# Five moves in a two-layer transformer kernel: the masks' load, one unit of an output projection, a residual add, a weight part, and a set of logarithms

## The chip, the cores and the metric

The kernel runs on one core of one Trainium2 chip. Its time is the device time of one execution in microseconds (us). The kernel before was timed in three runs: 1099.5, 1100.54 and 1105.1 us, median 1100.54 us. A further execution, recorded by the hardware profiler, is the one from which every duration below is read. Of the engines, TensorE (PE) multiplies matrices, VectorE (DVE) and ScalarE (ACT) work on elements, GpSimd (POOL) helps in one phase, and SyncE (SP) issues nearly all transfers (DMA).

## The reference, cut to what matters

Two transformer blocks run one after the other on 256 tokens of width 1024. What the change touches is, in the first block, the projections of the normed input, the cross-attention with its output projection and residual, and, in the second block, the forget gates of a gated linear recurrence:

```
h = rms_norm(x, mix_norm_g)
(..., f_q, f_k, f_v, f_g, s_q, s_k, s_v, gate_logits) = split_proj(h @ w_in)   # start of block 1
...
x = x + merged @ w_mix_out
q = rms_norm(x) @ w_xq ; k, v = rms_norm(mem) @ w_xkv          # 4 heads of 256
x = x + concat_h(softmax(q k^T / 16) v) @ w_xo                  # output projection "xo", residual
x = x + swiglu(rms_norm(x, ffn_norm_g), w_gate, w_up, w_down)   # feed-forward "a"
...
z = rms_norm_2(x) @ w_in_2                                      # start of block 2
f = lb + (1 - lb) * sigmoid(zf) ; logf = log(max(f, tiny)) ; k = (1 - lb) * sigmoid(-zf)
o = hgrn2_direction(q, k, v, logf)                              # forward and backward
```

The kernel computes the recurrence in levels; at levels 1 to 32 it merges scores under a 0/1 mask (`masks`, seven squares of 128x128), and this is the only use of the masks.

## The kernel before, in words

Every weight matrix is cut into **units**, at most 128 x 2048 floats (1 MB) each, numbered in the order in which they are used: fq 0 to 3, fk 4 and 5, fv 6 and 7, fg 8, sq 9 and 10, skv 11, cc 12 and 13, and so on. A unit passes through four engines. SP loads it into one of three `raw` buffers (`fetch`, L408), which is allowed when DVE has finished with unit n-3. ACT rounds it to a high part `whi` (`hi`, L1146), after PE has finished unit n-3. DVE subtracts to get the low part `wlo` (`lo`, L1717). PE then multiplies high by high, high by low and low by high (L531 for feature-major results, L588 for token-major ones, L633 and L635 for the first pair of a feed-forward). Activations are split into high and low parts in the same way (`ha`, `ox_hi`, `ox_lo`).

There is no scheduler. Each engine has a list of instructions written out by hand (`sync`, `tensor`, `scalar`, `vector`, `gpsimd`) and works through it in order; semaphores connect the five lists. On ACT and DVE a call such as `hi(U["xo0"][0][0] + 2)` stands two units ahead of PE, so it splits unit xo0 first half + 2, that is xo0's second half (the units of xo0 and xo1 alternate: xo0/0, xo1/0, xo0/1, xo1/1, then the feed-forward's first gate piece and first up piece).

The places of the change:

- **Start.** SP issues 448 KB of masks (`mk`, L433) behind many small loads and ahead of units 3 and 4. DVE turns them into bytes (`masks`, L1808) before the split of unit 8.
- **Cross-attention.** PE transposes the probabilities of head h (`x_probs`, L864), ACT copies them out (`xpt`), PE multiplies them with V (`x_values`, L876), ACT and DVE split the result (`ox_hi` L1345, `ox_lo` L1739). `x_values(2)` also needs the second half of V, which ACT copies out of PSUM (L1191) when PE has finished `mv1`. A unit of the first half of xo needs heads 0 and 1 only, one of the second half also heads 2 and 3.
- **Residual.** `add_half` adds the two halves of a PSUM bank to X (L1958) and then makes the low part of the next input (L1727). The feed-forward's first matmul (L633) waits for the low part of the first two rows of X, `("xo", 0)`.
- **Gates of block 2.** ACT computes sigmoids (L1491, L1492), scales the keys (L1499), loads another table and takes three logarithms for each of two directions (`half_logs`, L1505 to L1507). DVE does `half_gate` (L2108 to L2116) ahead of them and `half_log` (L2121) behind them. In between stand splits of the units hq0, zv and zu.

Of the kernel before, what the change touches and what calls it, by code (L numbers as in the profile page):

```python
# [95 lines left out]
def build(nc, d, out):  # L96
# [20 lines left out]
    masks = at("masks", [P, 7, P], U8, 91)  # L117
# [282 lines left out]
    def sync(e):  # L400
# [9 lines left out]
        def fetch_for(*names):  # L410
            for name in names:
                for u, _, _ in U[name]:
                    fetch(u + 2 + RAW)
# [19 lines left out]
        e.dma_start(mk[:, :, :], d["c_masks"].rearrange("p (l n) -> p l n", l=7)).then_inc(s_mk, 16)  # L433
# [7 lines left out]
        fetch_for("fk", "fv")  # L441
# [61 lines left out]
    def tensor(e):  # L503
# [400 lines left out]
        x_probs(3)  # L904
        x_values(2)
        unit("xo0", 0, OX, 1, ox_ready, a_evac.on(("mv0", 1)))
# [229 lines left out]
    def scalar(e):  # L1136
# [200 lines left out]
        def x_probs(h):  # L1337
            e.wait_ge(*pe_turn.on(("cross", h)))
            if h >= 2:
                e.wait_ge(*pe_val.on(("cross", h - 2)))  # L1340
            e.activation(xPT[h % 2][:, :, :], Tb, ACT.Copy).then_inc(*a_soft.up(("xpt", h)))
# [22 lines left out]
        x_probs(3)  # L1364
        ox_hi(2)
        hi(U["xo0"][0][0] + 2)
# [167 lines left out]
        tables("natural_log_exp_and_others")  # L1534
        half_logs(0, 0)
        hi(U["hq0"][1][0] + 2)
# [174 lines left out]
    def vector(e):  # L1711
# [95 lines left out]
        e.wait_ge(s_mk, 16)  # L1807
        e.tensor_copy(masks[:, :, :], mk[:, :, :]).then_inc(*v_stat.up("masks"))  # L1808
# [77 lines left out]
        rows_of("mem", Rm, 3)  # L1886
        e.wait_ge(*v_stat.on("cumulated"))
# [66 lines left out]
        def add_half(name, linear, s, i, gain, bias_ready=None):  # L1954
            for j in range(2):
                r = X[:, 4 * i + 2 * j:4 * i + 2 * j + 2, :]
                e.wait_ge(*half(linear, j))
                e.tensor_tensor(r, wide(banks[s][:, 512 * j:512 * j + 512]), r, ALU.add).then_inc(  # L1958
                    *v_evac.up((name, 2 * i + j)))
            for g in (2 * i, 2 * i + 1):  # L1960
                e.wait_ge(*v_evac.on((name, g)))
                scaled_lo(name, HA, g, lambda k: X[:, 2 * g + k, :], gain)
# [53 lines left out]
        lo(U["mv1"][1][0] + 2)  # L2016
        ox_lo(2)
        lo(U["xo0"][0][0] + 2)
# [3 lines left out]
        lo(U["xo1"][1][0] + 2)  # L2022
        add_half("xo", "xo0", 1, 0, lambda c: g_col("ffn_norm_g", c))
# [163 lines left out]
        half_gate(0, 1)  # L2187
        half_log(0, 0)
        lo(U["hq0"][1][0] + 2)
# [293 lines left out]
```

## Time and profile before

| what | value |
|---|---|
| three timed runs, median | 1100.54 us |
| the profiled execution, its own time | 1103.07 us |
| its span, first to last instruction | 1101.0 us |
| PE busy | 1081.7 us, 98% |
| DVE, ACT, POOL busy | 755.7, 600.8, 52.4 us |
| granted TensorE clock, mean | 0.998 of full |
| HBM traffic | 165 GB/s over the span |

2.07 us of the profiled execution's time lie outside its span. A page of the profile gives busy time by engine, a busy share by slice, the chain of work that ended last, and groups of instructions. Behind it stand the views used below: the waits of one engine, the timeline of a stretch, stretches with busy time and granted clock (windows), and the list of transfers.

### The profile page before, as it was taken

Reading aid. Unit: us, or ns where it says so; the run is one execution under the profiler, and the core shown is the slowest. Engines: PE = TensorE matmul, PEld = TensorE weight load, DVE = VectorE, ACT = ScalarE, POOL = GpSimd, SP = SyncE. Lnnn points to the kernel's source line nnn. Section 1 sums busy time; section 2 is a strip of 40 time slices with the busy share of each in tenths; the row PEclk is TensorE's granted clock in tenths of the full one; section 3 lists DMA queues with packets and bytes.
Section 4 is the critical chain, followed back from the end, with each engine's and each line's share of the span. In section 5 each row is a group of like instructions: output and inputs, shape, how many; then the busy total and the mean of one; then the engine's idle time right before and its main releaser. Section 6 shows DMA issues by size and latency. Waiting matters only on the chain.

```text
span 1101.0 us, 17157 instructions
## 1 busy us (share of the span) xinstructions
PE 1081.7 (98%) x7340; PEld 987.7 (90%) x7340; DVE 755.7 (69%) x875; ACT 600.8 (55%) x719; POOL 52.4 (5%) x32
## 2 busy tenths in 40 slices
PE   8999999999999999999999999999999999999997
PEld 7988888999998988888889899999999888888886
DVE  5465765567645468777558897579947888776456
ACT  5533355543534365455455986588655665555443
POOL 0000000000000000000000151005300000000000
PEclk9999999999999999999999999999999999999999
DMA  9954244465454347555556455444444637664641
GB/s 307 218 169 134 95 139 131 134 211 191 155 195 142 122 156 247 181 191 182 172 182 192 124 181 155 132 155 135 153 154 132 203 119 226 191 191 154 211 152 39
DMA packets 140075, 183.14 MB, mean 166 GB/s; under 512 B 14036, under 2 KB 90304, under 8 KB 140000
## 3 DMA queue, kind: packets, MB, share of 16 engines
q1 hardware_dynamic: 139736, 181.73, 52.4%
q8 instruction: 58, 0.95, 0.4%
q10 hardware_dynamic: 264, 0.32, 0.1%
q14 instruction: 17, 0.14, 0.0%
HBM read 180.79 MB, written 1.25 MB: 165 GB/s over the span
## 4 chain that ended last, share of the span: by engine, by line
PE 87%; ACT 6%; DVE 4%; issue 2%; DMA 1%; SPq 0%; DVEq 0%; ACTq 0%
PE ps L531 34%; PE ps L557 22%; PE ps L559 11%; PE ps L588 5%; PE ps L965 3%; DVE wlo L1717 2%; ACT whi L1146 2%; PE ps L633 1%; DMA raw<-in_w_in 1%; PE ps L1094 1%; PE ps L779 1%; PE ps L754 1%; PE ps L635 1%; PE ps L766 1%; ACT ha L1682 1%
## 5 line engine op out<-in xcount | busy, mean ns | idle before, releaser
L1717 DVE TENSOR_TENSOR wlo<-raw,whi 128x2048 fp32r<-128x2048 f32 (+2 forms) x170 | 379.3, 2234 | 184.0 <-ACT whi L1146 183.7
L1146 ACT ACTIVATE whi<-raw 128x2048 fp32r<-128x2048 f32 (+1 forms) x169 | 313.2, 1857 | 84.6 <-PE ps L531 39.7
L531 PE MATMUL ps<-ha,whi 128*128 128x256 f32 (+1 forms) x1728 | 316.8, 285 | 1.7 <-DVE wlo L1717 1.7
L531 PEld LDWEIGHTS ps<-ha,whi 128*128 128x128 f32 (+1 forms) x1728 | 268.4, 191 | 9.0 <-issue 7.3
L531 PE MATMUL ps<-ha,wlo 128*128 128x256 f32 (+1 forms) x864 | 244.3, 283 | 0.0
L557 PE MATMUL ps<-ha,whi 128*128 128x512 f32 x640 | 224.7, 396 | 0.6 <-DVE wlo L1717 0.6
L559 PE MATMUL ps<-ha,wlo 128*128 128x256 f32 x640 | 179.4, 280 | 0.0
L531 PEld LDWEIGHTS ps<-ha,wlo 128*128 128x128 f32 (+1 forms) x864 | 164.9, 191 | 0.2
L557 PEld LDWEIGHTS ps<-ha,whi 128*128 128x128 f32 x640 | 120.0, 187 | 29.0 <-issue 0.9
L557 PE MATMUL ps<-pr,whi 128*128 128x512 f32 x352 | 123.3, 395 | 0.0
L559 PEld LDWEIGHTS ps<-ha,wlo 128*128 128x128 f32 x640 | 120.9, 189 | 0.1
L559 PE MATMUL ps<-pr,wlo 128*128 128x256 f32 x352 | 98.7, 280 | 0.0
L557 PEld LDWEIGHTS ps<-pr,whi 128*128 128x128 f32 x352 | 66.0, 187 | 15.5
L2421 POOL TENSOR_TENSOR xf<-xf,pf 128x512 f32<-128x512 f32 x14 | 31.3, 2234 | 743.0 <-DVE pb L2121 698.5
L559 PEld LDWEIGHTS ps<-pr,wlo 128*128 128x128 f32 x352 | 66.5, 189 | 0.0
L1399 ACT ACTIVATE silu<-silu 128x512 f32<-128x512 f32 x22 | 13.9, 632 | 61.8 <-DVE silu L2047 61.8
L588 PE MATMUL ps<-whi,ha 128*128 128x512 f32 x128 | 40.0, 394 | 0.6 <-DVE wlo L1717 0.6
L1394 ACT ACTIVATE silu<-ps 128x512 f32<-128x512 f32 x22 | 13.1, 597 | 41.9 <-PE ps L559 37.9
L965 PE MATMUL ps<-qt,kt 128*128 128x128 f32 x256 | 32.6, 282 | 1.9 <-DVE am L2158 1.9
L965 PEld LDWEIGHTS ps<-qt,kt 128*128 128x128 f32 x256 | 31.5, 198 | 2.4 <-issue 2.1
L2144 DVE TENSOR_TENSOR qt<-qt,q 128x1024 f32<-128x1024 f32 x16 | 28.1, 1756 | 3.5 <-ACT qt L1442 3.4
L588 PEld LDWEIGHTS ps<-whi,ha 128*128 128x128 f32 x128 | 23.5, 188 | 5.6 <-DVE wlo L1717 1.0
(377 smaller groups left out, 1770.7 us busy)
## 6 DMA issues: line engine op xcount, KB each, us to landing
raw<-in_w_in SPq DMA_DIRECT2D x55, 1024.0 KB, 5.3
raw<-in_w_ffn_gate SPq DMA_DIRECT2D x11, 1024.0 KB, 5.2
raw<-in_w_ffn_up SPq DMA_DIRECT2D x11, 1024.0 KB, 5.2
raw<-in_w_gate SPq DMA_DIRECT2D x11, 1024.0 KB, 5.1
raw<-in_w_up SPq DMA_DIRECT2D x11, 1024.0 KB, 5.1
raw<-in_w_xkv SPq DMA_DIRECT2D x8, 1024.0 KB, 5.0
raw<-in_w_ffn_down SPq DMA_DIRECT2D x8, 1024.0 KB, 5.0
raw<-in_w_down SPq DMA_DIRECT2D x8, 1024.0 KB, 5.0
```

The source lines that it names most:

```text
L531: mm = e.matmul(ps[0:width, m * T:(m + 1) * T], a[:, kk, m * width:(m + 1) * width], b[:, off + k, :], start=k == 0 and j == 0 and m % 2 = ...
L557: e.matmul(banks[s][:, at_:at_ + 512], wh[:, kk, c], H[2][:, :, k, :], start=k == 0, stop=False, skip_group_check=True)
L559: mm = e.matmul(banks[s][:, at_ + T:at_ + 512], wl[:, kk, c], H[0][:, k, :], start=False, stop=k == K - 1, skip_group_check=True)
L588: mm = e.matmul(banks[s][:, t * 512:t * 512 + ncol], b[:, k, t * P:(t + 1) * P], a[:, kk, 0:ncol], start=k == 0 and j == 0, stop=k == 7 an ...
L633: e.matmul(banks[ss[i]][:, at_:at_ + 512], wh[:, k, c], H[2][:, :, k, :], start=k == 0, stop=False, skip_group_check=True)
L965: mm = e.matmul(Sb[w][:, m * P:(m + 1) * P], Kt[b][:, m, w * P:(w + 1) * P], Q_[:, m, wq_ * P:(wq_ + 1) * P], start=m == 0, stop=True, ski ...
L1146: e.activation(h, r, ACT.Copy).then_inc(*hi_done.up(n))
L1394: e.activation(silu[w][:, :, :], split_sums(ss[2 * (i % 2)])[1], ACT.Copy).then_inc(*a_evac.up(f"{b}g{i}"))
L1399: e.activation(silu[w][:, :, :], silu[w][:, :, :], ACT.Silu).then_inc(*a_stat.up((f"silu {b}", i)))
L1717: e.tensor_tensor(l, r, h.bitcast(F32), ALU.subtract).then_inc(*lo_done.up(n))
L2144: e.tensor_tensor(Qt[b][:, :, :], Qt[b][:, :, :], q[:, :, :], ALU.mult).then_inc(*v_mix.up(("qt", i, n)))
L2421: e.tensor_tensor(Xfl, Xfl, Pfu[:, :, h - 1:h].broadcast_to(shp), ALU.add).then_inc(*p_mix.up(("xf", i, n)))
```

## The change: what it does

1. SP's load of the masks moves from ahead of unit 3 to between units 10 and 11. DVE's conversion to bytes moves from ahead of the split of unit 8 to just ahead of the first attention work (behind the copy `rm`, L1752).
2. On PE the first unit of the output projection (xo0/0) moves ahead of `x_values(2)`. On ACT and DVE the split of xo0/1 moves ahead of the split of head 2's result.
3. On DVE the split of the feed-forward's first up piece (two units behind xo1/1) moves from ahead of the first residual add to between the add and the low parts that follow it.
4. On ACT the split of unit zv/1 moves ahead of the first three logarithms, on DVE ahead of the first addition of logarithms.

No instruction is added or removed.

```diff
@@ sync
-        e.dma_start(mk[:, :, :], d["c_masks"].rearrange("p (l n) -> p l n", l=7)).then_inc(s_mk, 16)
         fetch(3)
         fetch(4)
...
-        fetch_for("fk", "fv")
+        fetch_for("fk")
+        e.dma_start(mk[:, :, :], d["c_masks"].rearrange("p (l n) -> p l n", l=7)).then_inc(s_mk, 16)
+        fetch_for("fv")
@@ tensor
         x_probs(3)
+        unit("xo0", 0, OX, 1, ox_ready, a_evac.on(("mv0", 1)))
         x_values(2)
-        unit("xo0", 0, OX, 1, ox_ready, a_evac.on(("mv0", 1)))
         x_values(3)
@@ scalar
         x_probs(3)
+        hi(U["xo0"][0][0] + 2)
         ox_hi(2)
-        hi(U["xo0"][0][0] + 2)
...
         tables("natural_log_exp_and_others")
+        hi(U["hq0"][1][0] + 2)
         half_logs(0, 0)
-        hi(U["hq0"][1][0] + 2)
@@ vector
-        e.wait_ge(s_mk, 16)
-        e.tensor_copy(masks[:, :, :], mk[:, :, :]).then_inc(*v_stat.up("masks"))
         lo_for("fv")
...
         rows_of("mem", Rm, 3)
+        e.wait_ge(s_mk, 16)
+        e.tensor_copy(masks[:, :, :], mk[:, :, :]).then_inc(*v_stat.up("masks"))
...
+            if between is not None:
+                lo(between)
             for g in (2 * i, 2 * i + 1):
...
+        lo(U["xo0"][0][0] + 2)
         ox_lo(2)
-        lo(U["xo0"][0][0] + 2)
         ox_lo(3)
         lo(U["xo1"][0][0] + 2)
         lo(U["xo0"][1][0] + 2)
-        lo(U["xo1"][1][0] + 2)
-        add_half("xo", "xo0", 1, 0, lambda c: g_col("ffn_norm_g", c))
+        add_half("xo", "xo0", 1, 0, lambda c: g_col("ffn_norm_g", c), U["xo1"][1][0] + 2)
...
         half_gate(0, 1)
+        lo(U["hq0"][1][0] + 2)
         half_log(0, 0)
-        lo(U["hq0"][1][0] + 2)
```

The order of SP's transfers at the start. `raw_50 128x4x512` is unit 4, the first half of fk; `128x4x64 x8` are units 9 and 10. Before:

```order
L432 DMA sc<-in_forget_bias 8x1 x2
L433 DMA mk<-c_masks 128x896
L408 DMA raw_49<-in_w_in 128x2x512
L408 DMA raw_50<-in_w_in 128x4x512
L408 DMA raw_51<-in_w_in 128x4x512
```

and in the changed kernel:

```order
L432 DMA sc<-in_forget_bias 8x1 x2
L408 DMA raw_49<-in_w_in 128x2x512
L408 DMA raw_50<-in_w_in 128x4x512
L408 DMA raw_51<-in_w_in 128x4x512
L439 DMA m_tm<-in_mem 128x2x512
L408 DMA raw_49<-in_w_in 128x4x512
L439 DMA m_tm<-in_mem 128x2x512
L408 DMA raw_50<-in_w_in 128x4x512
L408 DMA raw_51<-in_w_in 128x8x8 x2
L408 DMA raw_49<-in_w_in 128x4x64 x8
L408 DMA raw_50<-in_w_in 128x4x64 x8
L441 DMA mk<-c_masks 128x896
```

The masks (`mk`) now stand behind unit 10 instead of ahead of unit 3.

DVE from the end of the cross-attention to the feed-forward. `xres` rows are the residual adds, `ha` rows the low parts, `wlo` rows the splits of weights. Before:

```order
L1717 TENSOR_TENSOR wlo_57<-raw_51,whi_54 128x2048
L1739 TENSOR_TENSOR ox_lo<-ps,ox_hi 128x512
L1717 TENSOR_TENSOR wlo_55<-raw_49,whi_52 128x2048
L1739 TENSOR_TENSOR ox_lo<-ps,ox_hi 128x512
L1717 TENSOR_TENSOR wlo_56<-raw_50,whi_53 128x2048
L1717 TENSOR_TENSOR wlo_57<-raw_51,whi_54 128x2048
L1717 TENSOR_TENSOR wlo_55<-raw_49,whi_52 128x2048
L1958 TENSOR_TENSOR xres<-ps,xres 128x512 x2
L1727 SCALAR_TENSOR_TENSOR ha<-xres,gc,ha 128x256 x4
```

and in the changed kernel:

```order
L1718 TENSOR_TENSOR wlo_57<-raw_51,whi_54 128x2048
L1718 TENSOR_TENSOR wlo_55<-raw_49,whi_52 128x2048
L1740 TENSOR_TENSOR ox_lo<-ps,ox_hi 128x512 x2
L1718 TENSOR_TENSOR wlo_56<-raw_50,whi_53 128x2048
L1718 TENSOR_TENSOR wlo_57<-raw_51,whi_54 128x2048
L1959 TENSOR_TENSOR xres<-ps,xres 128x512 x2
L1718 TENSOR_TENSOR wlo_55<-raw_49,whi_52 128x2048
L1728 SCALAR_TENSOR_TENSOR ha<-xres,gc,ha 128x256 x4
```

The first two adds now stand ahead of the last split, and the two splits of head 2's and head 3's results follow each other.

ACT at the logarithms of block 2. `pf`, `qt_133`, `xf` are the first direction, `pb`, `qt_134`, `xb` the second, `whi_53` is unit zv/1. Before:

```order
L1499 ACTIVATE kb<-kb,sc 128x256 x4
L1164 ACT_TABLE_LOAD
L1505 ACTIVATE pf<-pf,sc 128x1024
L1506 ACTIVATE qt_133<-qt_133,sc 128x1024
L1507 ACTIVATE xf<-xf,sc 128x1024
L1146 ACTIVATE whi_53<-raw_50 128x2048
L1505 ACTIVATE pb<-pb,sc 128x1024
L1506 ACTIVATE qt_134<-qt_134,sc 128x1024
L1507 ACTIVATE xb<-xb,sc 128x1024
```

and in the changed kernel:

```order
L1500 ACTIVATE kb<-kb,sc 128x256 x4
L1165 ACT_TABLE_LOAD
L1147 ACTIVATE whi_53<-raw_50 128x2048
L1506 ACTIVATE pf<-pf,sc 128x1024
L1507 ACTIVATE qt_133<-qt_133,sc 128x1024
L1508 ACTIVATE xf<-xf,sc 128x1024
L1506 ACTIVATE pb<-pb,sc 128x1024
L1507 ACTIVATE qt_134<-qt_134,sc 128x1024
L1508 ACTIVATE xb<-xb,sc 128x1024
```

The split stands three places earlier; the same nine rows remain.

## Rows read from the trace of the kernel before

**Rows 1.** The page, busy us by engine.

```profile
PE 1081.7 (98%) x7340; PEld 987.7 (90%) x7340; DVE 755.7 (69%) x875; ACT 600.8 (55%) x719; POOL 52.4 (5%) x32
```

**Rows 2.** Waits of PE: who for whom, us in total, times, longest.

```profile
PE ps L965 <- DVE am L2158: 1.9, 1, 1.9
PE ps L531 <- DVE wlo L1717: 1.7, 1, 1.7
...
PE ps L633 <- DVE ha L1727: 1.3, 1, 1.3
...
PE ps L876 <- issue: 1.0, 1, 1.0
```

**Rows 3.** Chain of waits: start us, us, what.

```profile
11.65 8.50 DMA raw<-in_w_in
...
24.56 11.76 PE ps L531 x96
```

**Rows 4.** Transfers of the first 50 us: issues, KB each, us to landing.

```profile
mk<-c_masks SPq DMA_DIRECT2D x1, 448.0 KB, 5.0
```

**Rows 5.** Windows: length, busy us by engine, clock, DMA share, GB/s.

```profile
10.00:20.00 10.00, 10.00 (x79) 9.04 (x78) 7.12 (x14) 6.25 (x13) 0.00 (x0) 1.00 1.02 348
23.00:25.00 2.00, 0.44 (x4) 0.47 (x5) 1.83 (x2) 1.55 (x1) 0.00 (x0) 1.00 0.94 291
```

**Rows 6.** Timeline, ACT at unit 4: start us, us, instruction, idle before.

```profile
20.17 1.91 ACT L1146 ACTIVATE whi<-raw 128x2048 fp32r<-128x2048 f32 x1 [1.81 <-DMA raw<-in_w_in]
```

**Rows 7.** Timeline, 41 to 73 us: the masks' conversion, and its new surroundings.

```profile
41.14 0.62 DVE L1808 CAST masks<-mk 128x896 uint8<-128x896 f32 x1
...
66.93 0.40 DVE L1834 TENSOR_SCALAR ca<-cumc,sc 16x256 f32<-16x256 f32 x1
...
60.24 3.72 ACT L1146 ACTIVATE whi<-raw 128x2048 fp32r<-128x2048 f32 x2
...
72.98 0.48 PE L750 MATMUL ps<-fk,fq 64*128 64x128 f32 x2
```

**Rows 8.** Timeline at the cross-attention's values, DVE, ACT and PE.

```profile
357.96 0.69 DVE L1739 TENSOR_TENSOR ox_lo<-ps,ox_hi 128x512 fp32r<-128x512 f32 x1 [1.04 <-ACT ox_hi L1345]
...
363.25 1.27 ACT L1191 ACTIVATE xv<-ps,sc 128x512 f32<-128x512 f32 x2 [3.03 <-PE ps L588]
...
364.62 1.96 PE L876 MATMUL ps<-xpt,xv 128*128 128x256 f32 x8 [0.97 <-issue]
```

**Rows 9.** Timeline at the residual add, DVE and PE.

```profile
387.61 2.29 DVE L1717 TENSOR_TENSOR wlo<-raw,whi 128x2048 fp32r<-128x2048 f32 x1 [3.47 <-ACT whi L1146]
389.82 1.28 DVE L1958 TENSOR_TENSOR xres<-ps,xres 128x512 f32<-128x512 f32 x2
391.56 1.67 DVE L1727 SCALAR_TENSOR_TENSOR ha<-xres,gc,ha 128x256 fp32r<-128x256 f32 x4 [0.46 <-ACT ha L1168]
...
392.59 0.47 PE L633 MATMUL ps<-ha,whi 128*128 128x512 f32 x1 [1.27 <-DVE ha L1727]
```

**Rows 10.** Timeline at the logarithms of block 2, ACT, DVE, PE, PE's weight loads.

```profile
599.87 1.15 ACT L1517 ACTIVATE ha<-h 128x512 fp32r<-128x512 f32 x2 [3.54 <-PE ps L531]
...
626.26 1.90 ACT L1146 ACTIVATE whi<-raw 128x2048 fp32r<-128x2048 f32 x1
...
626.39 1.22 DVE L2126 SCALAR_TENSOR_TENSOR q<-q_t,ps 128x1024 f32<-128x1024 f32 x1 [0.86 <-ACT q_t L1511]
628.20 2.38 DVE L1717 TENSOR_TENSOR wlo<-raw,whi 128x2048 fp32r<-128x2048 f32 x1 [0.58 <-ACT whi L1146]
...
623.19 0.73 PE L588 MATMUL ps<-whi,ha 128*128 128x512 f32 x2 [0.61 <-DVE wlo L1717]
...
630.70 0.30 PEld L531 LDWEIGHTS ps<-ha,whi 128*128 128x128 f32 x2 [0.17 <-issue]
```

**Rows 11.** Windows behind the wait of 1.9 us.

```profile
766.00:768.00 2.00, 1.66 (x10) 1.69 (x10) 2.00 (x3) 0.00 (x0) 1.91 (x2) 0.69 0.66 122
768.00:770.00 2.00, 2.00 (x11) 2.00 (x11) 2.00 (x3) 0.20 (x1) 0.00 (x0) 0.50 0.96 350
```

More of the change, by code:

```diff
@@ L1952, in vector, with add_half @@
             split_lo(("mg", g), MG[0][:, 4 * g:4 * g + 4, :], MG[1][:, 4 * g:4 * g + 4, :], mg[g][:, :, :], 0.5)
-        def add_half(name, linear, s, i, gain, bias_ready=None):
+        def add_half(name, linear, s, i, gain, between=None):
             for j in range(2):
```

## The prediction, made before the changed kernel was run

> **What bounds the kernel.** I read the page first: PE is busy 1081.7 us, 98% of the span of 1101.0 us [rows 1]. So the kernel is a string of matmuls with about 19 us of holes, and an edit that adds and removes nothing can only close or open holes. The second view is therefore the list of PE's waits [rows 2]. The reader is to see how short it is: one wait of 1.7 us for the low part of a weight unit (L531), one of 1.0 us before the values of the cross-attention (L876), one of 1.3 us for the first low part of the feed-forward (L633), one of 1.9 us in block 2. Third, the chain of waits and the timeline around each of them, to learn what it is that PE waits for and what stands behind it. The four edits each aim at one place. For each I ask two things: does the hole close, and is PE, arriving earlier at the next unit, let through?
>
> **Edit 1, the masks at the start.** The chain of waits goes through unit 4's load: it begins at 11.65 us and takes 8.50 us, and PE starts on the unit at 24.56 us, after the wait of 1.7 us [rows 2, 3]. ACT sat idle 1.81 us for that load [rows 6], so the load, and not ACT, is what is late. In front of it in SP's queue stand the masks, 448 KB [rows 4]. From 10 to 20 us the transfers moved 348 GB/s with all 16 DMA engines busy [rows 5]; 458,752 bytes at that rate are 1.32 us. ACT has 1.81 us of room to be early, DVE's split follows ACT, and PE has 1.7 us to gain, so I take the whole 1.3 us, and some 0.3 us of wait remain. Bounds: 0, if unit 4's load is held by its own latency and not by bytes (the masks alone took 5.0 us to land [rows 4], far more than 1.3), and 1.7 us, the whole wait. I choose 1.3 because the DMA share of 1.02 over that stretch speaks for bytes.
>
> The Trainium skill (DMA: Bandwidth & Descriptors, "Queues, rings and completion order") says that each DMA engine takes the descriptors of one ring in ring order; by that rule the masks' bytes must all go before unit 4's, which gives 1.3 us, while a queue in which later transfers may pass would give nearer to 0. No row here shows the order.
>
> The new places. SP now issues the masks between units 10 and 11, which it may do when DVE has split units 7 and 8; unit 8's split stood right behind the conversion at 41.14 us [rows 7], so the masks start near 40 us and delay unit 11 by the same 1.3 us. ACT takes units 11 and 12 at 60.24 us without idle time in front [rows 7], some 18 us after the earliest issue: hidden. The conversion (0.62 us) now waits for the masks on DVE near 66.9 us; with 5.0 us to land they are there 20 us before. Behind it on DVE are the two rows for head 0's decay (66.93 us, 0.40 each), which PE wants after 72.98 us [rows 7]: they end near 68.3 us instead of 67.7 us, with over 4 us of cover. Cost 0; if the cover were gone, 0.6 us.
>
> **Edit 2, xo0/0 ahead of head 2's values.** PE is free at 364.62 - 0.97 = 363.65 us, and waits for the copy of V's second half, which ends at 363.25 + 1.27 = 364.52 us [rows 8]. The unit that now stands there needs heads 0 and 1, whose last low part ended at 357.96 + 0.69 = 358.65 us [rows 8], a weight unit split long before and a bank already copied out. It starts at 363.65 us and takes 5.9 us (96 matmuls in 11.76 us [rows 3]), which covers the copy. What could be late next is head 3 for xo0/1: the values of heads 2 and 3 take 2 x 1.96 us at most [rows 8], so they end near 373.5 us, ACT and DVE need 0.6 and 0.7 us more, and PE reaches xo0/1 only one more unit later, near 379 us. Gain 1.0 us; bounds 0.9 and 1.0 us.
>
> **Edit 3, the residual add ahead of a split.** PE is free at 392.59 - 1.27 = 391.32 us. Before, DVE was idle 3.47 us in front of the split at 387.61 us, and the adds waited behind it until 389.82 us, the low parts until 391.56 us [rows 9]. The first add needs the middle, the second the end of xo0/1, which is one unit (5.9 us) before 391.32 us, so about 385.4 us. Both fit into the 3.47 us. The split keeps its place, since it waits for ACT, and ends at 389.90 us. ACT, which waited for the adds, makes the high parts right behind its own part of that unit, before DVE is back. The first two low parts, half of 1.67 us, end near 390.75 us. From low part to matmul it took 392.59 - (391.56 + 0.84) = 0.2 us [rows 9], so PE may start at 390.95 us: 0.4 us before it is free. The wait of 1.27 us goes whole. Next in line are the low parts for the other rows of X, and their adds come earlier too. Bounds: 0, if another wait takes the place, and 1.3 us.
>
> **Edit 4, zv/1's split ahead of the logarithms.** PE waited 0.61 us for it at 623.19 us [rows 10]. ACT's part comes three logarithms (about 3 us) earlier, so this wait goes. But PE then comes 0.61 us earlier to the scores and to unit zu/0. For zu/0, DVE's split ended at 628.20 + 2.38 = 630.58 us, ACT's part ran from 626.26 us without idle before it, and PE's weight load, which started at 630.70 us, already shows 0.17 us of idle [rows 10]. ACT had been working without a break since 599.87 us, when PE released it [rows 10]. That chain, 26.4 us of ACT until its part of zu/0, contains the same instructions in either order. So zu/0 starts when it started, and the 0.61 us become a wait in front of it. The scores in between need q, ready at 626.39 + 1.22 = 627.6 us [rows 10], about 0.5 us before PE asks. Gain 0.0 us; bounds 0.6 us, if the chain ends earlier than I think, and -0.2 us, if the swap makes it longer.
>
> **The sum.** 1.32 + 0.97 + 1.27 + 0.00 = 3.56 us. The profiled execution took 1103.07 us, 1101.0 us of span and 2.07 us around it; it would take 1099.5 us. The median of the timed runs, 1100.54 us, lies 2.5 us below the profiled one; with the same distance the forecast is 1097.0 us. The bounds together are 0.7 to 4.6 us, so 1095.9 to 1099.8 us.
>
> **Rivals.**
>
> *The masks were never in the way* (edit 1 gives nothing). For it: 5.0 us to land for 448 KB is mostly not bytes. Against: the DMA share of 1.02. Gain 2.2 us, 1098.3 us.
>
> *The fourth edit keeps its 0.6 us.* For it: DVE's addition of the first logarithms no longer stands around the split. Against: zu/0 hangs on ACT, and ACT's sum is unchanged. 1096.4 us.
>
> *The clock moves.* Behind the wait of 1.9 us the granted clock was 0.69 for 2 us and 0.50 (the 1.2 GHz level) for another 2 us [rows 11]: a loss of 2 x 0.31 + 2 x 0.50 = 1.6 us. Behind the wait of 1.7 us at the start it stayed at 1.00 [rows 5], so an idle of that size sometimes costs and sometimes not. If the changed kernel escapes one fall that the runs before had, it is 1095.4 us; with one fall more, 1098.6 us; it is slower than before from three falls more in the median run on (1101.8 us). For it: the timed runs before spread over 5.6 us. Against: the change removes idle time in front of PE in three places and lengthens none by more than 0.6 us.
>
> The Trainium skill (TensorE: Matmul & The Clock Gate, "What's actually happening") says that the gate's monitor runs free of the kernel's start, so one and the same wait can meet it in another phase. By that rule a shift of 3.6 us alone may give or take one such fall, which is the 1.6 us of this rival.
>
> *The masks are late in their new place* (slower). DVE stops in front of the conversion, and behind it stand head 0's decay, q of the sliding window and unit 13's split. It begins to cost when the masks land after about 71.5 us, and eats all of the gain at 75 us, 35 us after issue; at 77 us the time would be 1102.5 us. Against: 5.0 us to land at the start, in the busiest stretch.
>
> **Chances.** Forecast 62%, masks never in the way 12%, fourth edit pays 7%, one fall less or more 15%, slower by falls 3%, by late masks 1%. Half a per cent (5.5 us) is about what a measurement of this kernel can tell from no change. Even the upper bound of 4.6 us stays inside it; only with a fall less, or a lucky set of runs, does the time drop below 1095.0 us. So: faster by over 0.5% 12%, within 0.5% 84%, slower by over 0.5% 4%. The range, 1094.5 to 1100.3 us, holds the bounds of the sum, one fall in either direction, and nearly the spread of the medians.
>
> **What would show it.** In the changed profile: PE's wait near 24 us is 0.3 us instead of 1.7 us, and ACT's idle time for unit 4's load falls from 1.8 to about 0.5 us; no wait before the values at L876 and no wait before the first pair of the feed-forward; no wait for zv/1, but 0.6 to 0.8 us of idle before zu/0. PE busy stays at 1081 to 1082 us and the span falls to 1097.4 us. I am wrong if the first wait stays at 1.7 us, if the feed-forward waits for ACT's high parts, or if a new wait appears between 40 and 75 us.

## The result and the profile after

| | runs | median, us | lowest to highest |
|---|---|---|---|
| before, same chip and time | 22 | 1101.48 | 1098.05 to 1108.96 |
| changed kernel | 22 | 1098.11 | 1093.94 to 1103.95 |

The ratio of the changed kernel to the one before is 0.996, 95% interval 0.9946 to 0.9973. It lies inside the half per cent that was forecast; the medians are 3.4 us apart, and the predicted time was 1097.0 us. The profiled execution took 1099.06 us, its span is 1097.1 us, 3.9 us less than before. How much of the 3.9 us the change made is a question of its own. PE is 3.65 us ahead when it reaches feed-forward "a", but over 1 us of that belongs to one execution; the stretches that hold the edits are 2.8 us shorter.

The page of the changed kernel, busy us by engine, answers to [rows 1]:

```profile
PE 1080.7 (99%) x7340; PEld 986.2 (90%) x7340; DVE 754.8 (69%) x875; ACT 600.5 (55%) x719; POOL 55.6 (5%) x32
```

Its waits of PE answer to [rows 2]:

```profile
PE ps L966 <- DVE am L2160: 1.9, 1, 1.9
PE ps L598 <- DMA x_tm<-in_x: 1.2, 1, 1.2
PE ps L634 <- DVE ha L2375: 1.2, 1, 1.2
...
PE ps L532 <- DVE wlo L1718: 0.8, 1, 0.8
```

The waits at L876 (now L877) and for L1727 (now L1728) are not there any more. The row for L634 is the second block's (L2375 instead of L2373); it stood in the kernel before as well. The wait for a split (L532) is 0.8 us instead of 1.7 us, but it is not the same one: it lies at 623.87 us, in front of zu/0, where the prediction wanted 0.6 to 0.8 us. New is a wait of 1.2 us for the input x (0.23 us before), in front of everything that the change touches.

**The start.** ACT's timeline at unit 4 answers to [rows 6], and the chain of waits, with PE's timeline behind it, to [rows 3]:

```profile
18.97 1.90 ACT L1147 ACTIVATE whi<-raw 128x2048 fp32r<-128x2048 f32 x1
```

```profile
23.61 11.54 PE ps L532 x96
```

```profile
23.38 0.48 PE L532 MATMUL ps<-ha,whi 128*128 128x256 f32 x2
```

No idle time stands before ACT's split, in part because ACT itself comes 0.7 us later (the split of unit 3 in front of it starts at 18.02 us, before at 17.32 us). PE begins unit 4 at 23.38 us without a wait, 1.18 us earlier than before; the chain counts it from 23.61 us, where a small matmul that overlaps it ends. DVE converts the masks in their new place without waiting for them. The decay's row stands at 66.28 us, 0.65 us earlier than in [rows 7], while PE is 1.17 us ahead there: so it comes some 0.5 us later against PE, as worked out, and PE does not notice:

```profile
65.74 0.62 DVE L1887 CAST masks<-mk 128x896 uint8<-128x896 f32 x1
66.28 0.39 DVE L1833 TENSOR_SCALAR ca<-cumc,sc 16x256 f32<-16x256 f32 x1
```

**The cross-attention.** The chain of waits from the last transposes to the feed-forward's first matmul, to be laid beside [rows 8, 9]:

```profile
362.03 0.44 PE ps L865 x4
362.47 5.75 PE ps L532 x48
368.22 3.46 PE ps L877 x16
371.67 17.27 PE ps L532 x144
388.94 0.23 PE ps L634
```

xo0/0 (L532 x48, 5.75 us) stands where the wait of 0.97 us was. V's second half is copied meanwhile, from 362.07 to 363.34 us. The values of heads 2 and 3 (16 matmuls) and three more units follow without a hole, and the first pair of the feed-forward (L634) follows without one either. DVE's timeline shows why:

```profile
381.68 0.68 DVE L1959 TENSOR_TENSOR xres<-ps,xres 128x512 f32<-128x512 f32 x1
383.22 0.69 DVE L1959 TENSOR_TENSOR xres<-ps,xres 128x512 f32<-128x512 f32 x1 [0.86 <-PE ps L532]
385.23 2.29 DVE L1718 TENSOR_TENSOR wlo<-raw,whi 128x2048 fp32r<-128x2048 f32 x1 [1.31 <-ACT whi L1147]
387.44 1.67 DVE L1728 SCALAR_TENSOR_TENSOR ha<-xres,gc,ha 128x256 fp32r<-128x256 f32 x4
```

Both adds lie in the idle time that DVE had ahead of the split, and the split is still ahead of the low parts by its own length, as laid out. The first two low parts end at 387.44 + 0.84 = 388.28 us, 0.66 us before PE is there.

**The logarithms.** ACT, with the split of zv/1 ahead of the three logarithms, down to the split of zu/0, and PE in front of zu/0; beside [rows 10]:

```profile
609.00 1.92 ACT L1147 ACTIVATE whi<-raw 128x2048 fp32r<-128x2048 f32 x1
610.82 1.14 ACT L1506 ACTIVATE pf<-pf,sc 128x1024 f32<-128x1024 f32 x1
...
619.50 1.91 ACT L1147 ACTIVATE whi<-raw 128x2048 fp32r<-128x2048 f32 x1
...
623.87 0.47 PE L532 MATMUL ps<-ha,whi 128*128 128x256 f32 x2 [0.83 <-DVE wlo L1718]
```

PE no longer waits for zv/1, and waits 0.83 us for zu/0: the 0.61 us came back with 0.22 us on top, as idle time; whether the stretch is longer for it is measured further down.

**The whole difference.** Landmarks of PE, in us from the span's start, and how far the changed kernel is ahead:

| landmark | before | after | ahead |
|---|---|---|---|
| unit 4 | 24.56 | 23.38 | 1.18 |
| matmuls of block 1's attention (L606, L607) | 58.06 | 56.89 | 1.17 |
| xo1/0 (from the chain) | 374.06 | 371.67 | 2.39 |
| first pair of feed-forward "a" | 392.59 | 388.94 | 3.65 |
| zu/0 | 630.73 | 623.87 | 6.86 |
| the masked scores of block 2 | 766.34 | 759.46 | 6.88 |
| first pair of feed-forward "b" | 878.67 | 870.16 | 8.51 |
| last projection of feed-forward "b" | 1085.76 | 1080.46 | 5.30 |
| end of the span | 1101.0 | 1097.1 | 3.9 |

Up to the feed-forward "a" it is 3.65 us, near the 3.56 us that were forecast, but not by the same terms: 1.18 us come from the start, and 2.5 us from the cross-attention and the residual, where the two waits come to 2.24 us. Behind it the lead nearly doubles, grows once more to 8.51 us and then shrinks to less than half, in places that the change does not touch. Two things do this. One is a pace. Windows of 100 us in each of the two feed-forwards, PE alone (length, busy us with the number of matmuls, clock, DMA share, GB/s), before:

```profile
430.00:530.00 100.00, 100.00 (x571) 1.00 0.56 178
900.00:1000.00 100.00, 100.00 (x579) 1.00 0.61 192
```

and after:

```profile
430.00:530.00 100.00, 100.00 (x581) 1.00 0.58 185
900.00:1000.00 100.00, 100.00 (x568) 1.00 0.61 194
```

PE is busy without a hole at a full granted clock in all four, and yet the same matmuls go by at 571 or 581 and 568 or 579 per 100 us. PE's lead grows by 2.9 us over the first feed-forward (from its second pair, 393.02 and 389.13 us, to the column sums behind it, 587.30 and 580.53 us) and shrinks by 3.2 us over the second (8.51 us at its first pair, 5.31 us at the wait of 1.0 us behind it, 1070.19 and 1064.88 us). The other is the clock. Before, it fell behind the wait at 766 us [rows 11], and the lead grew by 1.6 us; after, it did not fall there:

```profile
759.00:761.00 2.00, 1.54 (x14) 1.57 (x15) 2.00 (x3) 0.10 (x1) 2.00 (x2) 1.00 0.54 109
761.00:763.00 2.00, 2.00 (x20) 2.00 (x19) 2.00 (x3) 1.42 (x3) 0.03 (x1) 1.00 0.99 345
```

It fell instead behind the last wait, of 2.7 us, at 1080 us (granted clock 0.51 from 1080 to 1082 us, 1.00 before the wait). The last projection in the chains of waits, before and after:

```profile
1085.76 11.52 PE ps L1094 x72
```

```profile
1080.46 12.86 PE ps L1095 x72
```

That is 1.34 us given back for one fall, against about 1.6 us saved for the other.

### The profile page after: what moved, and what is told of

It reads as the page before. It is cut to its first block, busy times and chain, and to the rows that moved or that the text cites. A ratio compares the mean times of both kernels' runs of the same rounds, so it can differ in the third digit from the quotient of the medians.

```text
span 1097.1 us, 17157 instructions
## 1 busy us (share of the span) xinstructions
PE 1080.7 (99%) x7340; PEld 986.2 (90%) x7340; DVE 754.8 (69%) x875; ACT 600.5 (55%) x719; POOL 55.6 (5%) x32
## 4 chain that ended last, share of the span: by engine, by line
PE 88%; ACT 6%; DVE 4%; issue 2%; DMA 1%; SPq 0%; DVEq 0%; ACTq 0%
PE ps L532 36%; PE ps L558 22%; PE ps L560 11%; PE ps L589 5%; PE ps L966 2%; ACT whi L1147 1%; PE ps L634 1%; PE ps L1095 1%; DVE wlo L1718 1%; PE ps L780 1%; PE ps L755 1%; PE ps L636 1%; PE ps L767 1%; ACT ha L1683 1%; PE ps L855 1%
## 5 line engine op out<-in xcount | busy, mean ns | idle before, releaser
L532 PE MATMUL ps<-ha,whi 128*128 128x256 f32 (+1 forms) x1728 | 316.5, 285 | 0.8 <-DVE wlo L1718 0.8
L532 PEld LDWEIGHTS ps<-ha,whi 128*128 128x128 f32 (+1 forms) x1728 | 268.1, 191 | 7.9 <-issue 6.3
L532 PE MATMUL ps<-ha,wlo 128*128 128x256 f32 (+1 forms) x864 | 244.2, 283 | 0.0
L532 PEld LDWEIGHTS ps<-ha,wlo 128*128 128x128 f32 (+1 forms) x864 | 164.7, 191 | 0.2
L2423 POOL TENSOR_TENSOR xf<-xf,pf 128x512 f32<-128x512 f32 x14 | 34.5, 2463 | 731.7 <-DVE pb L2123 691.6
```

The source lines that it names most:

```text
L532: mm = e.matmul(ps[0:width, m * T:(m + 1) * T], a[:, kk, m * width:(m + 1) * width], b[:, off + k, :], start=k == 0 and j == 0 and m % 2 = ...
L2423: e.tensor_tensor(Xfl, Xfl, Pfu[:, :, h - 1:h].broadcast_to(shp), ALU.add).then_inc(*p_mix.up(("xf", i, n)))
```

## The experiments

Two theories stand against each other. *By the trace*: each edit is worth the wait that it removes, 1.3 or 1.7 us for the masks, 1.0, 1.3 and 0. *By the execution*: a wait that one profiled execution shows may not be the kernel's, and pace and clock, which change from execution to execution, make more of a difference than any single edit. Each time stands beside runs of the kernel before on the same chip: 31 on the chip of e1 to e4, 28 on the chip of e5, e6, e9 and the changed kernel's second timing, 17 on the chip of e7, e8, e10 and the kernel before timed against itself. The three chips are different ones.

### Each edit alone

```diff
 # e1: edit 1 alone (the masks' load behind unit 10, their conversion ahead of the attention)
 # e2: edit 2 alone
         x_probs(3)
+        unit("xo0", 0, OX, 1, ox_ready, a_evac.on(("mv0", 1)))
         x_values(2)
 # e3: edit 3 alone
+        add_half("xo", "xo0", 1, 0, lambda c: g_col("ffn_norm_g", c), U["xo1"][1][0] + 2)
 # e4: edit 4 alone
         tables("natural_log_exp_and_others")
+        hi(U["hq0"][1][0] + 2)
         half_logs(0, 0)
```

> Edit 1 alone. Theory (bytes): the 448 KB ahead of unit 4 held it back. PE's wait before the first fk unit falls from 1.7 us to at most 0.4 us, ACT's idle time for unit 4's load from 1.8 us to under 0.6 us, the masks' conversion sits near 67 us and no new wait of PE appears before 75 us; the other holes (1.0 us before the values, 1.3 us before the feed-forward) stay. Total about 1.3 to 1.7 us less than before. Rival (latency): the load of unit 4 takes as long as before, the wait stays near 1.7 us, total unchanged. In the two feed-forwards the number of matmuls per 20 us (115 or 117 to 118) may go either way: it is expected to be the run's and not the edit's.

> Edit 2 alone. Theory: the wait of 1.0 us before the values of head 2 is gone and nothing takes its place; the stretch from the last transposes of the probabilities to the end of the output projection is 1.0 us shorter, the wait of 1.3 us before the feed-forward stays. Total 1.0 us less. Rival (given back): head 3's result comes too late for the second half of xo and PE waits there for what it saved; total unchanged.

> Edit 3 alone. Theory: the wait of 1.3 us before the first pair of the feed-forward is gone, with low parts ready 0.4 us before PE asks; total 1.3 us less. Rival (new wait): ACT's high parts or the split between the add and the low parts end last and leave 0.5 us or more of the wait.

> Edit 4 alone. Theory (ACT's chain): the wait of 0.6 us for unit zv/1 is gone, and a wait of 0.7 to 0.9 us stands before unit zu/0 instead; the time from the end of fb0's first unit to the start of zu/0 stays 30.8 us; total unchanged to 0.1 us. Rival: the wait goes for good, zu/0 starts 0.6 us earlier against fb0, total 0.6 us less.

| kernel | median (10 runs each) | ratio, 95% | PE's wait at unit 4 | at head 2's values | at the first pair | at zv/1 | at zu/0 |
|---|---|---|---|---|---|---|---|
| before (31 runs) | 1103.1 | | 1.66 | 0.97 | 1.27 | 0.61 | none |
| e1 | 1104.74 | 1.0018 (0.9999 to 1.0036) | none | 0.97 | 1.27 | 0.61 | none |
| e2 | 1103.37 | 0.9999 (0.9977 to 1.0022) | 0.18 | none | 1.26 | 0.61 | none |
| e3 | 1101.24 | 0.9991 (0.9969 to 1.0014) | none | 0.97 | none | 0.61 | none |
| e4 | 1103.11 | 1.0004 (0.998 to 1.0028) | none | 0.97 | 1.27 | none | 0.83 |

The waits fall apart as cleanly as one could wish: each edit removes its own and leaves the others. No edit alone can be told from no change by its time, which is no surprise for 1 us; e1's interval leaves at most 0.1 us of gain, though, where 1.3 to 1.7 us were expected. The surprise is the column of unit 4. In e2, e3 and e4 the masks stand ahead of unit 4 exactly as before, and the wait on which edit 1's term rested is not there. ACT at unit 4 in e3:

```profile
18.56 1.91 ACT L1146 ACTIVATE whi<-raw 128x2048 fp32r<-128x2048 f32 x1 [0.28 <-DMA raw<-in_w_in]
```

0.28 us of idle time for the load instead of 1.81 us [rows 6], with the same transfers in the same order.

### The masks loaded twice, and the kernels traced again

```diff
 # e5: the kernel before, and ahead of units 3 and 4 a second load of the same 448 KB
         e.dma_start(mk[:, :, :], d["c_masks"]...).then_inc(s_mk, 16)
+        e.dma_start(mk2[:, :, :], d["c_masks"]...).then_inc(s_mk, 16)
```

> The kernel before with a second load of the same 448 KB right behind the first, into spare room, both ahead of unit 3. If bytes ahead of unit 4 delay it, unit 4 is 1.3 us later than with one load and PE's wait before fk is 1.3 us or more longer than the 0.0 to 0.2 us of the traces of edits 2, 3 and 4 alone (so 1.3 us or more). If its own latency rules, the wait stays at 0.2 us or, as in the first trace, at 1.7 us at most.

A single execution took 1107.43 us, span 1105.5 us. ACT's splits of units 3 and 4 (one row), and of unit 5:

```profile
18.52 2.96 ACT L1148 ACTIVATE whi<-raw 128x1024 fp32r<-128x1024 f32 x2
...
24.62 1.91 ACT L1148 ACTIVATE whi<-raw 128x2048 fp32r<-128x2048 f32 x1 [3.13 <-DMA raw<-in_w_in]
```

Units 3 and 4 follow each other within 2.96 us, so ACT hardly waited for unit 4, whose split was done at 21.48 us; before, it was done at 20.17 + 1.91 = 22.08 us [rows 6], with half the masks' bytes ahead. Against e2 (18.70 + 1.92 = 20.62 us) it is 0.86 us later, and SP issued the load 0.71 us later (at 10.68 instead of 9.97 us). So 448 KB more cost unit 4 0.9 us at the very most, and much of that is the time at which it was issued. PE did not wait for unit 4 here, but it also came 1.0 us later than usual (23.95 us against 22.9 us), since the input x had come late; on time, it would have waited about 1 us (21.48 + 2.48 = 23.96 us, with the 2.48 us that lay between the end of ACT's split and PE's start before). A second 448 KB would thus begin to cost something; the first fits into the slack. The idle time of 3.13 us at unit 5, which starts 2 to 3 us later here than in the two traces of the kernel before (24.62 us against 22.64 and 21.30 us), caused no wait of PE.

> The kernel before, unchanged, timed against itself and traced a second time. It says what a ratio of this kernel's runs can tell from no change, and whether the wait of 1.66 us for unit 4, on which a third of the forecast gain rested, belongs to the kernel or to one execution. If to the kernel: 1.3 to 1.8 us again near 24 us. If to one execution (the four traces with the masks ahead of unit 4 since then had 0 to 0.2 us): 0 to 0.5 us. The ratio to itself should be 1 within 0.002; the pace of the matmuls in the first feed-forward is 571 or 581 per 100 us, and which of the two is not the kernel's doing if this trace or the next one of the same text differs from the 571 of the first.

> The changed kernel once more, for a second trace and a time beside edits 2 and 3 alone. Theory: the holes are the same as in its first trace (none at unit fk, the values and the feed-forward, 0.8 us before zu/0); the number of matmuls per 20 us in the two feed-forwards (117 to 118 in the first, 115 in the second in its first trace) can be different, since it is the run's and not the kernel's. Rival: the pace repeats (fast in the first, slow in the second), and so is a property of the order.

The kernel before, traced a second time, shows ACT idle for 0.24 us and no wait of PE at unit 4. All fourteen traces together, this one with the double load among them: with the masks ahead of unit 4 there are nine, with waits of 1.66, 0.18 and seven times none; with the masks moved there are five, with 0.72, 0.45 and three times none. The averages are equal, 0.2 us. Nor does unit 4's load land sooner each time without the masks ahead: ACT starts on it, after idle time, at 19.07 and 19.22 us in e6 and e8, against 18.63, 18.70 and 18.56 us in three traces that have the masks ahead (the kernel before again, e2, e3); in the changed kernel's second trace it was there by 18.20 us. Edit 1 does not pay, and the 1.66 us were one execution's.

Timed against itself, the kernel before gave 1101.54 us (12 runs) beside 1104.64 us (17 runs): a ratio of 0.9973, interval 0.9955 to 0.9991, for the same text. Such an interval does not hold all of what differs between two sets of runs, and 0.3% is nothing to build on. The changed kernel against 28 runs of before (1103.76 us) gave 1101.83 us, 0.9977 (0.9957 to 0.9996), 1.5 us above the end of my range, where the first comparison had 0.996; the kernel before itself was 2.3 us slower there than in the first comparison.

The traces put a better number on the change. The sum of PE's waits over the whole span, in us:

| | first trace | second trace |
|---|---|---|
| before | 15.17 | 13.52 |
| changed | 12.15 | 11.52 |

The first pair differs by the wait at unit 4 and the input's lateness as well. The second has neither (0.42 and 0.35 us for the input), and differs by 2.00 us: 0.96 + 1.27 + 0.61 - 0.83 = 2.01 us.

But idle time is not all that a wait costs. Take the stretch from the last transposes of the probabilities to the second pair of feed-forward "a", which holds edits 2 and 3, before and after:

```profile
363.05 0.60 PE L864 MATMUL ps<-ident,xl 128*128 128x128 f32 x4
...
393.02 0.40 PE L633 MATMUL ps<-ha,whi 128*128 128x512 f32 x1
```

```profile
361.87 0.60 PE L865 MATMUL ps<-ident,xl 128*128 128x128 f32 x4
...
389.13 0.40 PE L634 MATMUL ps<-ha,whi 128*128 128x512 f32 x1
```

It takes 29.97 us before and 27.26 us after: 2.7 us less, and not 2.24 us. All fourteen traces agree to 0.01 us: 29.96 or 29.97 us without edits 2 and 3, 28.76 us with edit 2 alone, 28.46 us with edit 3 alone, 27.26 or 27.27 us with both. So the wait of 0.97 us cost 1.20 us and the wait of 1.27 us cost 1.50 us. The first matmuls behind a wait take longer: in the chains of waits the values of a head take 1.96 us behind the wait and 1.73 us without one. At edit 3 the first two pairs start 0.43 us apart behind the wait and 0.35 us apart without one; where the rest of its 0.23 us lies is not worked out.

The stretch with the logarithms runs from the last column sums in front of them (L615) to the projection behind the second scores (L588):

```profile
587.30 1.03 PE L615 MATMUL ps<-npre,ones 128*128 128x256 f32 x4
...
645.80 0.70 PE L588 MATMUL ps<-whi,ha 128*128 128x512 f32 x2
```

```profile
580.53 1.03 PE L616 MATMUL ps<-npre,ones 128*128 128x256 f32 x4
...
638.95 0.70 PE L589 MATMUL ps<-whi,ha 128*128 128x512 f32 x2
```

It takes 58.50 us before and 58.42 us after; the seven traces with the old order have 58.48 to 58.50 us, the three with the new one (e4 and both of the changed kernel) 58.40 to 58.42 us. Edit 4 gains 0.1 us, though its wait is 0.22 us longer. The whole change is worth 2.8 us.

### Edits 2 and 3 without 1 and 4

> Edits 2 and 3 together, the masks and the logarithms as before. Theory (the wait of 1.7 us at the start belonged to one profiled execution: it is missing in the traces of edits 2, 3 and 4 alone, which leave the masks where they were): the trace shows unit fk starting near 23 us with a wait under 0.4 us although the masks are ahead, no wait before the values and none before the feed-forward, and the total is 2.2 us below before, as good as the whole change. Rival (the masks count in the median): the whole change is a further 1.3 us or more faster than this one, on the same chip.

1098.8 us (11 runs), ratio 0.9955 (0.9935 to 0.9975): no worse than the changed kernel in either of its comparisons. Its trace has neither the wait at the values nor the one at the first pair, none at unit 4, and 0.61 us at zv/1 where the changed kernel has 0.83 us at zu/0. The changed kernel beside it took 3.0 us more (1101.83 us), which no wait explains; in the two traces the first feed-forward's matmuls go at 581 and 571 per 100 us. The other two edits can be left out.

### ACT's chain made shorter, not reordered

If edit 4 gave nothing because the chain on ACT from PE's release to zu/0 holds the same instructions in either order, then taking an instruction out of it must give what the exchange could not.

```diff
 # e6: in the changed kernel, the keys' scaling of direction 0, first half, goes from ACT to DVE
 # e7: the same in the kernel before
 # e8: as e6, and the keys of direction 1, second half, too
 # e10: as e8, on edits 2 and 3 alone
@@ scalar, half_keys
+            if (i, j) in ((0, 0), (1, 1)):
+                return
...
@@ vector, half_gate
-            e.wait_ge(*a_mix.on(("k", i, j)))
+            if (i, j) in ((0, 0), (1, 1)):
+                for m in range(4):
+                    c = 8 * j + 4 * i + m
+                    mm = e.tensor_scalar(k_[:, m, :], k_[:, m, :], omb[:, c:c + 1], None, ALU.mult)
+                mm.then_inc(*v_mix.up(("k", i, j)))
+                e.wait_ge(*v_mix.on(("k", i, j)))
+            else:
+                e.wait_ge(*a_mix.on(("k", i, j)))
```

The list of halves is that of e8 and e10; in e6 and e7 it holds (0, 0) alone.

> The changed kernel, with the scaling of the first direction's keys (four instructions, 1.7 us of ACT) moved to DVE, into an idle stretch of 1.5 us. Theory (ACT's chain sets zu/0): ACT reaches the logarithms, q's tanh and zu/0's part 1.7 us earlier, and the wait of 0.8 us before zu/0 is gone; total 0.8 us less than the changed kernel. Rival (DVE or the scores set it): the wait stays, or turns up before the scores.

1099.34 us (12 runs), ratio 0.9962 (0.9945 to 0.9979). No wait for zv/1 and none for zu/0 (but 0.45 us at unit 4, with the masks out of the way). The stretch with the logarithms takes 57.34 us, 1.1 us less than in the changed kernel. DVE does the four scalings in 1.13 us where ACT took 1.69 us, and has room for them:

```profile
604.02 1.13 DVE L2122 TENSOR_SCALAR kf<-kf,sc 128x256 f32<-128x256 f32 x4
```

> The kernel before, with the first half's keys of direction 0 scaled on DVE instead of ACT; nothing else. Looked at for its trace. Theory: ACT's chain from PE's release to the splits of zv/1 and zu/0 is 1.7 us shorter, so both waits (0.61 us for zv/1, and the 0.2 us behind it at zu/0) are gone with the logarithms in their old order; the others stay (0.97 us before head 2's values, 1.27 us before the feed-forward's first pair). Rival: DVE's extra 1.1 us makes its part of zv/1 late instead, and 0.3 us or more of wait stays. Near 23 us a further look at how much the kernel before waits for unit 4: 1.7 us if its first trace was typical, 0 to 0.2 us if it was not.

A single execution took 1102.61 us. With the logarithms in their old order both waits are gone as well, and the stretch takes the same 57.34 us. So the order hardly mattered (0.1 us), and the length of ACT's chain did.

> The changed kernel, with the scaling of the keys (four activations, 1.70 us) moved from ACT to DVE (four of 0.28 us) for two of the four key halves: the first of direction 0 as in the run before this one, and the last of direction 1, whose ACT chain runs into the largest wait that is left (1.87 us, PE for DVE's masked scores in block 2). Theory (ACT's chain sets when PE goes on): the wait before zu/0 stays at 0, and since ACT reaches its splits 1.6 us earlier and DVE was idle 1.9 us for ACT at the logarithms, the wait of 1.9 us shrinks to 0.3 to 0.7 us. Against the changed kernel that is 0.8 + 1.3 = 2.1 us, ratio to the kernel before 0.995 (forecast 1097.5 to 1098.5 us where the kernel before has 1103). Rival (DVE is the bound there): DVE runs without a break from 739 us to the wait, at up to 3.2 us a split while GpSimd works; the 1.1 us added to DVE then eats the gain and the wait stays at 1.8 to 2.0 us; ratio 0.997.

1096.39 us (6 runs), ratio 0.992 (0.9895 to 0.9946), 1.1 us below the forecast of 1097.5 to 1098.5 us. The largest of the waits in the middle of the kernel, for DVE's masked scores, shrinks from 1.87 to 0.43 us. DVE at the logarithms ahead of it:

```profile
733.21 1.22 DVE L2132 TENSOR_TENSOR pf<-pf,qt 128x1024 f32<-128x1024 f32 x1
734.83 1.23 DVE L2132 TENSOR_TENSOR pb<-pb,qt 128x1024 f32<-128x1024 f32 x1 [0.41 <-ACT qt L1509]
```

In the changed kernel DVE was idle there for 1.90 us, for ACT:

```profile
737.28 1.23 DVE L2123 TENSOR_TENSOR pb<-pb,qt 128x1024 f32<-128x1024 f32 x1 [1.90 <-ACT qt L1507]
```

DVE runs without a longer break from there to the wait, and it looks like the bound; it is ACT that lets it start 1.5 us late. The wait for the first low part of feed-forward "b" grows from 1.16 to 1.51 us, but little is given back: from the masked scores to the wait of 1.0 us in front of the last stretch but one (1062.62 us) it takes 305.62 us, where the changed kernel takes 305.42 and 305.46 us and e6 305.59 us.

> Only the moves that removed waits in every trace so far (xo0/0 ahead of head 2's values, the residual add ahead of the split), with the keys of the same two halves scaled on DVE; the masks' load and the logarithms stay where the kernel before has them. Theory (the masks' load is not in the way, and a shorter ACT chain does what the logarithms' exchange could not): waits are those of the run with both key halves moved, with 0 to 0.5 us near 23 us; no wait for zv/1 and none for zu/0 although the logarithms stand ahead of the split, since ACT comes 1.7 us earlier. Ratio equal to that run's within 0.002. Rival (the masks matter): 1.3 us slower than that run, with a wait of 1.3 us or more near 23 us. Rival (zv/1 still waits): 0.6 us at the unit behind the logarithms.

1094.28 us (6 runs), ratio 0.9912 (0.9885 to 0.9939), span 1094.0 us; within 0.001 of the run with all four edits. All waits of PE over 0.15 us that are left:

```profile
PE ps L1094 <- ACT tg L1701: 2.7, 1, 2.7
PE ps L633 <- DVE ha L2383: 1.5, 1, 1.5
PE ps L676 <- DVE ones L1774: 1.1, 1, 1.1
PE ps L1094 <- DVE ha L2383: 1.0, 1, 1.0
PE ps L557 <- DVE wlo L1719: 0.6, 1, 0.6
PE ps L606 <- DVE n_tm L1749: 0.6, 1, 0.6
PE ps L597 <- DMA x_tm<-in_x: 0.6, 1, 0.6
PE ps L965 <- DVE am L2168: 0.4, 1, 0.4
PE ps L645 <- DVE nsq L2321: 0.2, 1, 0.2
```

8.79 us of idle time instead of 13.52 us. Masks and logarithms stand where they stood before. This is the best version that the runs point to, and it beats both kernels: its interval lies below 0.9946, where the changed kernel's first one begins. The waits that its edits remove are 0.96 + 1.27 + 0.61 + 1.45 - 0.35 = 3.9 us; most of the rest of the 4.7 us is a wait in the first 10 us (1.15 us, for the first split) that other traces have at 0 to 1.4 us. In elapsed time the edits are worth more: 2.7 us in the stretch of edits 2 and 3, 1.15 us in the one with the logarithms and 1.6 us from there to the masked scores (118.92 us instead of 120.53 us), some 5.3 us with what is given back. The medians differ by 10 us, and what is above that is not settled. Falls of the clock behind the wait that is now 0.4 us, and the 0.3% by which a kernel differs from itself, are large enough for it, but the timed runs have no trace.

## Why the prediction was right, and where it was not

**The forecast of 1097.0 us** stands 1.1 us beside the first median and 4.8 us beside the second. Its sign is right, and the mechanism holds for edits 2, 3 and 4. Its size is partly luck: edit 1 was put 1.3 us too high, and the others came out 0.5 us above their terms, which leaves 2.8 us of the 3.56 us. That the profiled pair differs by 3.9 us is luck too, since pace and clock moved it by 4.5 us one way (2.9 + 1.6) and by as much the other (3.2 + 1.3).

**Edit 1, the term that failed.** I took 1.32 us, "because the DMA share of 1.02 over that stretch speaks for bytes", and kept 0 as a bound. Measured over fourteen traces it is 0.0 us. The rival "the masks were never in the way" (12%) is what the runs show. The reasoning on bytes may even hold, at a cost below 0.9 us for unit 4, but without them the load came sooner in one trace (by 18.20 us) and later in two (19.07 and 19.22 us) than the 18.6 us of three traces with them. What was wrong is the cover: I read the wait of 1.66 us [rows 2] as the kernel's, and it was a late load of one execution. Hints were there. ACT was idle 1.81 us for a load that [rows 3] has at 8.50 us, of which bytes ahead explained only 1.3 us; the rest, which I left as "some 0.3 us", had no cause in the program. The expectation "wait near 24 us 0.3 instead of 1.7 us" came out as no wait, and looked like a success. Only the kernels with the masks left in place showed that it was none.

The new places cost nothing, as worked out: the masks were issued at 42.07 us (worked out: near 40 us) and landed in 4.1 us, and the conversion at 65.74 us waited for nothing. The rival "late in their new place" did not happen.

**Edit 2.** 0.97 us forecast. The wait of 0.97 us is gone (e2), with nothing late behind it, and the stretch is 1.20 us shorter. The term took a wait at its idle time, and left out that the first matmuls behind it are slower. ox_lo of head 3 ended at 372.34 + 0.69 = 373.03 us, as expected.

**Edit 3.** 1.27 us forecast. The wait of 1.27 us is gone (e3), and the stretch is 1.50 us shorter: the same kind of excess over the idle time. PE was to find the low parts 0.4 us before it is free, and found them 0.66 us before.

**Edit 4.** 0.00 us forecast, 0.1 us less measured. The traces of e4 and of both changed kernels have a wait of 0.83 us for one of 0.61 us, which looks like the bound of 0.2 us worse, and is none: the stretch is not longer. e6 and e7 show the reason given, ACT's chain, by shortening it. That the fourth edit keeps its 0.6 us (7%) is refuted.

**The clock.** The rival was priced at 1.6 us a fall and given 15% either way. In the first pair of traces one fall went (at 766 us) and another came (at 1080 us), which I had not looked at. The last projection took 11.50 to 11.52 us in eight traces, 12.85 to 13.09 us in five, and 14.29 us in one, behind the same wait of 2.7 us. That is 0, 1.3 to 1.6, or 2.8 us, in kernels that do the same there, and the second traces of the two kernels differ from the first. The fourteen traces show such falls in two more places: behind the wait of 1.9 us at the masked scores in four (before, e2, e4, e5), and near 74 us in seven (both second traces, e1, e5, e7, e9, e10). The one near 74 us has no wait of PE over 0.15 us ahead of it since the one at 56 to 58 us. The longest of them, in the second trace of the kernel before, lasted 7 us, a loss of 3.4 us:

```profile
73.00:80.00 7.00, 7.00 (x31) 6.35 (x32) 4.30 (x11) 2.79 (x5) 0.00 (x0) 0.51 0.11 44
```

So an execution carries none (e3) to two of these falls, up to 5 us together. The 15% were given to one fall more or less in the medians, where such falls average out; for a pair of single traces it is far too little.

The Trainium skill (TensorE: Matmul & The Clock Gate, "What's actually happening") says that the gate's monitor runs free of the kernel's start; the traces agree with it, in that one wait of one length at one place gives three outcomes.

**The pace** was in no part of the prediction, and made the largest shifts between the two traces, 2.9 us one way and 3.2 us the other.

## What to carry to other kernels

Before a wait is counted as a gain, look whether it is the kernel's: trace the same text a second time, and distrust a wait for a DMA that is longer than what the program puts in front of it. Moving an instruction along an engine that works without a break moves the wait and does not shorten it; take the instruction off that engine, onto one that is idle for it. For effects near 0.2% take two landmarks that both kernels share, around the edit, and compare the time between them in several traces: here it repeats to 0.01 us, while the sum of the waits leaves out 0.2 us for each wait that goes. Time the old kernel against itself too, since the medians alone put two sets of runs of one text 0.3% apart.

## What was not expected of the hardware

The matmuls of the feed-forwards go at two paces with the granted clock at 1.00 and no hole. In the first feed-forward the window from 430 to 530 us holds 571 matmuls in nine traces and 581 in five (after, e1, e6, e8, e9). In the second, from 900 to 1000 us, it is 567 to 569 in eleven and 579 in three (before, e7, e10). One text has both: the changed kernel 581 and then, traced again, 571; the kernel before 579 and then 568. The DMA share is 0.55 to 0.58 and 0.59 to 0.63 in all of them. What sets the pace stays open. It is worth 2.6 to 3.2 us in the first feed-forward (191.75 to 191.83 us from the first pair to the column sums behind it, or 194.3 to 195.0 us) and some 3.2 us in the second. Together with the clock's falls it is large enough for the 10 us by which timed runs of one kernel differ, but those have no trace.

A wait costs more than its idle time: 0.23 us more at each of the two that edits 2 and 3 remove, in every trace. And the clock can fall where PE has hardly waited: near 74 us, in seven traces of fourteen.
